# Waits at seven places of a two-layer transformer kernel: what is asked for when, and the order of the output products

## The reference, cut to what matters

```
x = x + 0.5 * swiglu(rmsnorm(x))
h = rmsnorm(x);  aq, ak, av, bq, bk, bv, cq = split(h @ w_in)
o_a = diff_attention(aq, ak, av)       # A: difference of two maps, rmsnorm of the heads
o_b = chunk_band_attention(bq, bk, bv) # B: with a bias table
o_c = memory_attention(cq, mk, mv)     # C
y = sum_n sigmoid(h @ w_gate[n] + b) * (o_n @ w_branch[n])
x = x + y @ w_out                      # "wo"
x = x + 0.5 * swiglu(rmsnorm(x)); x = rmsnorm(x, final_norm)
```

```
z = rms_norm(x, g_mix) @ w_in_2
k_c, v_c = gelu(blocks(kc + pos) @ w1) @ w2  # compression of keys and of values
y_nsa = gated sum of compressed, selected and window attention    # N0, N1
y_rnn = gelu(g_rnn) * rg_lru(conv(x_rnn))
y_x   = cross_attention(q_x, mem) @ w_xo                          # X
y = gm0 * y_nsa + gm1 * y_rnn + gm2 * y_x    # gates m0, m1, m2g
x = x + y @ w_o                              # "wo2"
x = x + relu(rms_norm(x) @ w_up)**2 @ w_down; out = rms_norm(x, g_final)
```

## Time and profile before

| | |
|---|---|
| runs | 2305.72, 2310.17, 2310.17 us |
| profiled execution | 2307.07 us |
| its span | 2304.6 us, 29999 instructions |
| busy: DVE, ACT, POOL | 1228.3, 972.9, 150.8 us |
| granted clock of TensorE, mean | 0.991 |

### The profile page before, as it was taken

How to read it: one execution, slowest core, us unless ns; L and a number is a source line. 1 busy time by engine, 2 the same in 40 slices (tenths; PEclk the granted TensorE clock), 3 DMA queues, 4 the chain that set the end, 5 groups by cost and what they waited for, 6 DMA issues and landing times.

```text
span 2304.6 us, 29999 instructions
## 1 busy us (share of the span) xinstructions
PE 2257.2 (98%) x11038; PEld 1799.9 (78%) x11038; DVE 1228.3 (53%) x2220; ACT 972.9 (42%) x1579; POOL 150.8 (7%) x119
## 2 busy tenths in 40 slices
PE   8999999999999999999999999999999999999998
PEld 6888888867768888888888887786555787888887
DVE  7444446674475556444435647835888554432432
ACT  7332223456585333332223322633888443322322
POOL 2000002100110001000002420000000001000011
PEclk9999999999999999999999999999999999999999
DMA  6323322312202233222322372222000232332231
GB/s 243 107 86 96 109 84 83 107 55 70 95 11 91 86 106 110 91 91 85 116 91 80 111 232 82 70 80 74 2 2 11 83 110 92 96 105 91 91 110 55
DMA packets 213646, 206.81 MB, mean 90 GB/s; under 512 B 4880, under 2 KB 194576, under 8 KB 213296
## 3 DMA queue, kind: packets, MB, share of 16 engines
q1 hardware_dynamic: 210544, 192.31, 26.4%
q0 software_dynamic: 3008, 13.24, 1.7%
HBM read 199.25 MB, written 4.19 MB: 88 GB/s over the span
## 4 chain that ended last, share of the span: by engine, by line
PE 86%; DVE 7%; ACT 3%; issue 2%; DMA 1%; POOL 0%; SPq 0%; ACTq 0%; DVEq 0%; POOLq 0%
PE ps L917 25%; PE ps L919 25%; PE ps L918 25%; PE ps L766 3%; PE ps L778 2%; DVE Sm L869 2%; PE ps L1137 1%; DVE wlo L655 1%; DMA wraw<-in_w_in 1%; ACT whi L648 1%; PE ps L1046 1%; PE ps L1177 1%; PE ps L1202 1%; DVE Sm L903 0%; PE ps L1156 0%
## 5 line engine op out<-in xcount | busy, mean ns | idle before, releaser
L917 PE MATMUL ps<-hH,whi 128*128 128x512 f32 x1528 | 601.0, 393 | 4.0 <-DVE wlo L655 2.2
L919 PE MATMUL ps<-hH,wlo 128*128 128x512 f32 x1528 | 594.7, 389 | 0.0
L918 PE MATMUL ps<-hL,whi 128*128 128x512 f32 x1528 | 594.6, 389 | 0.0
L655 DVE TENSOR_TENSOR wlo<-wraw,whi 128x2048 fp32r<-128x2048 f32 x192 | 441.2, 2298 | 285.3 <-ACT whi L648 285.3
L648 ACT ACTIVATE whi<-wraw 128x2048 fp32r<-128x2048 f32 x192 | 367.0, 1911 | 508.9 <-PE ps L919 499.7
L917 PEld LDWEIGHTS ps<-hH,whi 128*128 128x128 f32 x1528 | 286.3, 187 | 67.9 <-issue 5.3
L918 PEld LDWEIGHTS ps<-hL,whi 128*128 128x128 f32 x1528 | 286.3, 187 | 62.5 <-issue 3.1
L919 PEld LDWEIGHTS ps<-hH,wlo 128*128 128x128 f32 x1528 | 286.3, 187 | 60.5
L917 PE MATMUL ps<-gH,whi 128*128 128x512 f32 x608 | 237.2, 390 | 0.0
L919 PE MATMUL ps<-gH,wlo 128*128 128x512 f32 x608 | 236.6, 389 | 0.0
L918 PE MATMUL ps<-gL,whi 128*128 128x512 f32 x608 | 236.6, 389 | 0.0
(11 more groups left out here) (371 smaller groups left out, 2668.4 us busy)
## 6 DMA issues: line engine op xcount, KB each, us to landing
wraw<-in_w_in SPq DMA_DIRECT2D x45, 1024.0 KB, 5.0
wraw<-in_ffn_wg SPq DMA_DIRECT2D x22, 1024.0 KB, 5.1
wraw<-in_ffn_wu SPq DMA_DIRECT2D x22, 1024.0 KB, 5.1
wraw<-in_w_up SPq DMA_DIRECT2D x16, 1024.0 KB, 5.2
wraw<-in_w_down SPq DMA_DIRECT2D x16, 1024.0 KB, 5.8
wraw<-in_ffn_wd SPq DMA_DIRECT2D x16, 768.0 KB, 4.5
wraw<-in_w_gate SPq DMA_DIRECT2D x12, 1024.0 KB, 4.9
wraw<-in_ffn_wd SPq DMA_DIRECT2D x16, 640.0 KB, 4.3
```

The lines of the kernel that those rows point to most:

```text
L655: dve.tensor_tensor(wlo[s][:, :], wraw[s][:, :], f32(whi[s][:, :]), ALU.subtract).then_inc(w_lo[s], 1)
L917: pe.matmul(o, lh, rh, start=start, stop=False)
L918: pe.matmul(o, lh, rl, start=False, stop=False)
L919: return pe.matmul(o, ll, rh, start=False, stop=stop)
```

## The change

Seven edits of order and waits; no product, copy or transfer is added or left out.

1. The compression weights get a semaphore for keys and one for values. POOL issues the keys' set, then the eight `Z` copies of the keys, then the values' set, then the other eight copies. PE waits for each set where it uses it.
2. On DVE, `scaled(6)` stands ahead of `merge1(4)` and no longer behind it.
3. to 5. `attention_over` is split. After A, C and X, PE waits for the turns at once, and for the outputs only before it first writes bank 2 or 3.
6. and 7. `wo` and `wo2` go through `pe_late`: in the first round slot 0 chunks 0 to 5, slot 1 chunks 0 and 1, slot 0 chunks 6 and 7, then slot 1 chunks 2 to 7 for bank 2 and for bank 3. The second round has each bank's eight chunks in one piece.

```diff
+            def compression(m):
+                n = "kv"[m]
+                pool.dma_start(w1c[m][:, :, :], ...).then_inc(cmp_in[m], 16)
+                pool.dma_start(w2c[:, m, :, :], ...).then_inc(cmp_in[m], 16)
+
+            compression(0)
             for m in range(2):
                 for g in range(4):
                     ...
+                if m == 0:
+                    compression(1)
@@
-        def attention_over(eng, name):
+        def turns_over(eng, name):
             A = attn_at[name]
             eng.wait_ge(t_free, T_RING + A["T0"] + A["its"] * A["turns"])
+        def outputs_over(eng, name):
+            A = attn_at[name]
             eng.wait_ge(o_free, O_RING + A["O0"] + A["its"] * A["groups"])
@@
+        def pe_late(pe, S, rh, rl, ready):
+            def product(i, s, g, kc):
+                at = kc * 256 + g * P
+                b = 2 * s + g
+                mm = mm3(pe, ps[b][:, :], whi[s][:, at:at + P], wlo[s][:, at:at + P], rh(i, s, kc), rl(i, s, kc), kc == 0, kc == 7)
+                if kc == 7:
+                    mm.then_inc(mm_full[b], 1)
+            def banks(i, s):
+                pe.wait_ge(w_lo[s], i + (S["k0"] + 1))
+                for b in (2 * s, 2 * s + 1):
+                    pe.wait_ge(mm_free[b], free_before(S, b, i))
+            for s, k0, k1 in ((0, 0, 6), (1, 0, 2), (0, 6, 8)):
+                if k0 == 0:
+                    banks(0, s)
+                for kc in range(k0, k1):
+                    if s == 0:
+                        ready(pe, 0, kc)
+                    for g in range(2):
+                        product(0, s, g, kc)
+            for g in range(2):
+                for kc in range(2, 8):
+                    product(0, 1, g, kc)
+            for i in range(1, S["its"]):
+                ...
@@ pe_toks
+                        if ("bank", t) in between:
+                            between["bank", t]()
@@ pe_compress
-            pe.wait_ge(cmp_in, 64)
             for m in range(2):
+                pe.wait_ge(cmp_in[m], 32)
@@ after A, C and X
-            attention_over(pe, "A")
+            turns_over(pe, "A")
+            ... bq: between={("bank", 2): lambda: outputs_over(pe, "A"), ...}
-            attention_over(pe, "C")
+            turns_over(pe, "C")
+            ... gate0: if s == 1 and kc == 0 and n == 0: outputs_over(pe_, "C")
-            attention_over(pe, "X")
+            turns_over(pe, "X")
+            ... m0: between={(0, 0, 1, 7): lambda: outputs_over(pe, "X")}
@@ DVE, m1
             merge1(3)
+            scaled(6)
             merge1(4)
-            scaled(6)
             scaled(7)
```

More of the change, by code:

```diff
@@ L423, in build @@
         sp_out, spilled, spill_back = sem("sp_out"), sem("spilled"), sem("spill_back")
-        cmp_in, rg_in = sem("cmp_in"), sem("rg_in")
+        cmp_in, rg_in = [sem(f"cmp_in{m}") for m in range(2)], sem("rg_in")
         bias_in = [sem(f"bias_in{h}") for h in range(2)]
@@ L558, in _ @@
             pool.dma_start(spill, xT[:, :, :].rearrange("p c t -> p (c t)")).then_inc(spilled, 16)
-            for m, n in enumerate("kv"):
-                pool.dma_start(w1c[m][:, :, :], a[f"w_cmp_{n}1_2"][0].rearrange("(m p) n -> p m n", p=P)).then_inc(cmp_in, 16)
-                pool.dma_start(w2c[:, m, :, :], a[f"w_cmp_{n}2_2"][0].rearrange("(c p) n -> p c n", p=P)).then_inc(cmp_in, 16)
+            def compression(m):
+                n = "kv"[m]
+                pool.dma_start(w1c[m][:, :, :], a[f"w_cmp_{n}1_2"][0].rearrange("(m p) n -> p m n", p=P)).then_inc(cmp_in[m], 16)
+                pool.dma_start(w2c[:, m, :, :], a[f"w_cmp_{n}2_2"][0].rearrange("(c p) n -> p c n", p=P)).then_inc(cmp_in[m], 16)
+            compression(0)
             for m in range(2):
@@ L970, in pe_cols @@
                 loop(pe, S["its"], body)
+        def pe_late(pe, S, rh, rl, ready):
[21 more added lines that the diff above has]
+            for i in range(1, S["its"]):
+                for s in range(2):
+                    banks(i, s)
+                    for g in range(2):
+                        for kc in range(8):
+                            product(i, s, g, kc)
         def pe_toks(pe, S, i, lh, ll, ready, tiles=TT, fresh=False, between={}):
@@ L1268, in _ @@
                          lambda e, n: KT[rows_of(e.m), e.i * 2 + e.h, 0:n], pv_a, "ak", lambda e: 2 * e.i + e.h)
-            attention_over(pe, "A")
-            pe_toks(pe, stages["bq"], 0, hH, hL, no_wait, between=turn("oa", lambda t, c: oT[:, c, t * P:(t + 1) * P]))
+            turns_over(pe, "A")
+            pe_toks(pe, stages["bq"], 0, hH, hL, no_wait,
+                    between={("bank", 2): lambda: outputs_over(pe, "A"),
+                             **turn("oa", lambda t, c: oT[:, c, t * P:(t + 1) * P])})
             pe_toks(pe, stages["bk"], 0, hH, hL, no_wait, between=turn("bq", q_cols))
@@ L1285, in ready @@
                     if s == 1:
+                        if kc == 0 and n == 0:
+                            outputs_over(pe_, "C")
                         pe_.wait_ge(o_lo, 4 * n + kc + 1)
@@ L1289, in _ @@
                         lambda i, s, kc, n=n: hL[:, kc, :] if s == 0 else oL[n % 2][:, kc, :], ready)
-            pe_cols(pe, stages["wo"], QUAD, lambda i, s, kc: yH[:, kc, :], lambda i, s, kc: yL[:, kc, :],
-                    hset_ready("y1"), fresh=True)
+            pe_late(pe, stages["wo"], lambda i, s, kc: yH[:, kc, :], lambda i, s, kc: yL[:, kc, :], hset_ready("y1"))
             pe_ffn(pe, 2, "ffn2", {("chunk", 3): lambda: pe_sums(pe, "ffn2"),
@@ L1342, in _ @@
                          lambda e: 3 if e.kind == "X" else {"c": 0, "s": 0, "w": 2}[e.m] + int(e.name[1]))
-            attention_over(pe, "X")
-            pe_cols(pe, stages["m0"], QUAD, hh, hl, no_wait)
+            turns_over(pe, "X")
+            pe_cols(pe, stages["m0"], QUAD, hh, hl, no_wait, between={(0, 0, 1, 7): lambda: outputs_over(pe, "X")})
             S = stages["xo"]
@@ L1356, in _ @@
             pe_cols(pe, stages["m2g"], QUAD, hh, hl, no_wait)
-            pe_cols(pe, stages["wo2"], QUAD, lambda i, s, kc: y2H[:, kc, :], lambda i, s, kc: y2L[:, kc, :],
-                    hset_ready("y2"), fresh=True)
+            pe_late(pe, stages["wo2"], lambda i, s, kc: y2H[:, kc, :], lambda i, s, kc: y2L[:, kc, :], hset_ready("y2"))
             for half in range(2):
```

## The result

The changed kernel takes 2311.03 us (median of 20 runs, 2306.1 to 2314.86), the kernel before 2307.35 (20 runs, 2303.06 to 2310.17): ratio 1.0015, 95% interval [1.0009, 1.0021], so it is slower by about 3.5 us (2.1 to 4.8). The forecast was +0.4. The profiled execution took 2310.18 us, its span 2308.2, against 2307.07 and 2304.6: +3.6 in the span.

What follows compares the result with a forecast made beforehand. TensorE is busy for 98% of the span, so only its standing still counts. Terms -2.5 + 0 + 0.2 + 2.7 + 0 = +0.4 us on the readings' average 2308.3 gave 2308.7 us, range 2304.2 to 2313.0.

Steps and rivals of the forecast that it cites:

- Ends of attention: After attentions A, C and X: PE no longer stops for ACT's copy of the last output bank, -2.5 us.
- Rival 4: Ends of attention: hand-overs bring nothing, because PE waited for issue and not for ACT; 2310.0 us, chance 0.08.
- Scaling ahead of a merge: In `m1`: the wait for bank 2 goes, but PE then waits about 1.5 us for the split; 0 us.
- The compression weights: At the compression: the weight tile keeps its rate beside `Z` copies, as queues share equally by packets; +0.2 us.
- `wo`: First layer's output products: slot 0 ends 12 products later, PE's wait for its split grows to about 3.2; +2.7 us.
- Rival 2: At `wo`: DVE's chain does not move, so the sum is -2.3 or -3.8, 2304.8 to 2303.3 us; chance 0.10.
- The clock behind that wait: After the longer wait at `wo`: the summed forecast counted no loss from a lower TensorE clock.
- Rival 1: At `wo`: the 3.2 us wait drops the clock to 1.2 GHz, costing 1.7 or 6.5 us more; chance 0.27.
- `wo2`: Second layer's output products: the wait for `y2L` stays, and slack covers slot 0's 2.7 us later split; 0 us.
- The sum: Whole kernel: all five terms together, +0.4 us, 2307.5 us on the profile's scale.

Runs made afterwards that it cites:

- after_again: The changed kernel itself, unaltered, run once more for a second profile: span 2307.5 us.
- after_wo_old: The changed kernel with the output products of the first layer (`wo`) back in their old order: 2307.18 us, ratio 1.0002 to the kernel before.
- after_filled: The changed kernel plus twelve unused products into a spare bank while PE waits at `wo`: 2308.11 us, ratio 1.0005 to the kernel before.
- ends_wo: The kernel before with only the three moved waits after attentions A, C, X and the new order of `wo`: 2308.32 us, ratio 1.0002.

## Why the prediction was wrong, step by step

- **Ends of attention, -2.5: right, a little small.** The hand-overs gave -1.0, -1.3 and about -0.8, -3.1 together and more than the -2.6 that was to be the most. The term took the printed idle time (0.73, 1.06, 0.74), and a stop costs more than that, since the first products behind it start further apart. The -0.6 between them, by the clock in the light work, was in no term. Rival 4 is out: the waits were ACT's copy.
- **Scaling ahead of a merge, 0: right**, and for the reason given: the chain ran through the split. The new wait was put at 1.5 and is 1.7.
- **The compression weights, +0.2: the step that failed**, in its size and in a clock fall that it left out. Six profiles with the edit have steps of 0.5 to 4.3, mean 1.9; eight without it have -0.6 to 0.6, mean -0.1. The difference is 2.0 us, and the ratio of its own kernel says 2.3. The cost has two parts.

  First, PE's wait behind the tile is 1.9 to 4.1 us with the edit and 1.3 before: +1.2 in the mean. Second, behind the waits of 2.4, 2.5 and 4.1 us (after_again, after_wo_old, after_filled) the clock falls for 3.4 us, 1.4 to 1.6 more each time, +0.8 in the mean of six; behind those of 1.9, 2.2 and 2.3 it holds.

  The mechanism of the term, the share of the two queues, was right: it is one to one in every window. But from the share I took the pace. In 2 us each queue sends about 155 to 185 packets with weights on both and 123 to 161 beside `Z` copies, and only 94 to 120 in the slowest 2 us where POOL's queue goes over from one kind to the other, at both changes of every profile with the edit. The tile is 1 MB in packets of 1 KB (0.12 MB, 122 packets), so some 1000; a change that costs it 40 to 60 of them costs 0.5 to 0.8 us at 160 in 2 us.

  Without the edit one such change falls into the tile's last microseconds, with 132 in its slowest 2 us before and 117 to 137 in the nine profiles; the edit puts two into its middle. The tile takes 21.5 to 23.7 us with the edit (mean 22.2) and 20.4 to 21.5 without it (nine, mean 20.9): 1.3 us, which is the longer wait. The earlier trace rows were two windows without a change; the edit's own two weren't in the sum, and the clock was weighed at `wo` alone.
- **`wo`, +2.7: right**, 2.70 to 2.73 in all seven profiles with that order and the old softplus, filled or not. Rival 2 is out.
- **The clock behind that wait: forecast without, and it fell.** Rival 1 was the case, at its short price of 1.7 against 1.6 measured. The forecast had it at 0.27, on the ground that dense products follow. They follow in all six profiles with the wait, with the fall and without it, so that ground decides nothing.
- **`wo2`, 0: right.** The split moved by 2.7 and the next was back, the wait for `y2L` stayed at 1.3.
- **The sum.** With the sizes measured: -1.0 - 1.3 - 0.8 - 0.6 + 2.7 + 1.6 + 2.0 = +2.6, inside the measured 2.1 to 4.8. From +0.4 it is off by +1.8 at the compression, +1.6 at the clock, -1.2 at the ends. The timed kernels with one edit give -3.5 + 3.9 + 2.3 = +2.7, which agrees.

Open: why a wait that begins 276 us after the earlier fall drops the clock and one of the same length at 278 us doesn't. The wait is 3.1 to 3.2 us with and without the ends of attention, and PE is gapless for the 15 us before it. That the 1.6 us are in the timed medians isn't shown either: ends_wo's ratio is that of the sum of its parts without it, within 2 us. That the clock's losses as a whole are in the changed kernel's timed runs has some support: its 20 executions have a mean granted clock of 0.9906, and those of the kernel before in the four sets of the experiments 0.9915 to 0.9923 (some 0.0003 of noise in each). That is 2 to 4 us of its time, at no known place.

## What to carry to other kernels

A wait that nobody's data needs is free to move; an order of products isn't: whoever finishes a bank later must first follow what hangs on that bank, here the sum, the rounding, a small softplus and only then the next weights. Look for what stands in that chain and needn't: taking the softplus and one merge out of it was worth 2.8 us, nearly as much as the three ends of attention (3.1). A wait that grows has a second price, the clock behind it, and that isn't to be weighed at the longest wait alone. And read a shared queue's pace in every kind of window that the moved transfers will make, the change from one kind to the next too, before a share of one to one is taken for a rate.

## What was unexpected of the hardware

- The pace of two DMA queues that alternate packet by packet is not fixed: about 155 to 185 packets each in 2 us with weights on both, 123 to 161 beside copies within the on-chip memory, 94 to 120 in the slowest 2 us where one queue goes over from one kind to the other. The Trainium skill, "DMA: Bandwidth & Descriptors", section "Queues, rings and completion order", has the change by packets, and every window agrees; how long such a turn takes is what these runs add.
- The same 3.2 us of idle time in dense work dropped the granted clock to 0.50 for 3.4 us in three of three profiles and not at all in three of three others, which differ in three hand-overs of about 1 us far ahead, and with them in when the wait comes. At the compression waits of 2.4, 2.5 and 4.1 us dropped it, and those of 1.9, 2.2 and 2.3 us didn't. Twelve spare products in the gap at `wo` kept it at 1.00.
